# A hybrid decoder trunk on one core: GpSimd's 512-column subtractions in the gate/up units issued as two of 256

## What is computed

```
def swiglu(h, w_gu, w_down):
    gate, up = jnp.split(h @ w_gu, 2, axis=-1)
    return (jax.nn.silu(gate) * up) @ w_down

x = x + 0.5 * swiglu(rmsnorm(x, n1), ffn1_gu, ffn1_down)
... (mixer: gated linear attention and sliding-window attention)
x = x + 0.5 * swiglu(rmsnorm(x, n2), ffn2_gu, ffn2_down)
```

## Time and profile before

| | |
|---|---|
| time, median of 3 | 2162.82 us (2158.97 to 2165.57) |
| the profiled execution's own time | 2163.97 us |
| its span, first to last instruction | 2162.2 us |
| mean granted TensorE clock | 0.976 |
| PE, DVE, ACT, POOL busy | 95%, 66%, 39%, 45% of the span |
| POOL's 512-column subtractions (L535) | 360: 278.0 + 200.4 + 63.1 us busy |

### The profile page before, as it was taken

One profiled execution on the slowest core, in us unless ns is written; L12 is line 12 of the kernel. 1 busy time (PEld: TensorE's weight loads), 2 busy tenths in 40 slices (PEclk: granted clock), 3 DMA queues, 4 the chain that ended last, 5 costly groups with the idle time before them and its releaser, 6 DMA issues.

```text
span 2162.2 us, 41578 instructions
## 1 busy us (share of the span) xinstructions
PE 2044.2 (95%) x15854; PEld 1989.8 (92%) x15854; DVE 1425.0 (66%) x1853; ACT 846.8 (39%) x1469; POOL 980.0 (45%) x549
## 2 busy tenths in 40 slices
PE   6899999999999999999999999999999998999996
PEld 6899999998889999999998999999898998999996
DVE  8899932386348899952288997226754498999323
ACT  4455532235233445542235555222541334555321
POOL 3466654332203366664426666444321134666541
PEclk9999999999879999999999999999997999999998
DMA  3322242421212322242223222423220213222421
GB/s 121 124 93 92 82 153 94 133 79 50 81 52 71 114 88 92 92 143 98 97 74 125 92 88 99 143 95 127 69 91 30 68 63 134 88 92 78 159 98 61
DMA packets 86277, 206.74 MB, mean 96 GB/s; under 512 B 12240, under 2 KB 13936, under 8 KB 85616
## 3 DMA queue, kind: packets, MB, share of 16 engines
q1 hardware_dynamic: 78336, 192.06, 26.5%
q10 hardware_dynamic: 7824, 13.01, 1.8%
HBM read 191.20 MB, written 15.86 MB: 96 GB/s over the span
## 4 chain that ended last, share of the span: by engine, by line
issue 51%; PE 18%; POOL 16%; DVE 10%; DMA 2%; ACT 1%; DVEq 1%; POOLq 0%; SPq 0%; ACTq 0%
PE ps L565 13%; POOL w_lo L527 11%; POOL w_lo L535 6%; PE ps L591 5%; DVE ps L1356 3%; DMA w_raw<-stream 1%; DVE act L1391 1%; DVE b_tmp L1401 1%; DVE ssum L1447 1%; DVE s_tmp L1356 1%; DVE g_buf L1420 1%; DVE rs L1318 0%; DVE rhs L1413 0%; DVE b_tmp L1405 0%; DVE ssum L1458 0%
## 5 line engine op out<-in xcount | busy, mean ns | idle before, releaser
L591 PE MATMUL ps<-rhs,w_hi 128*128 128x272 f32 x4032 | 782.9, 291 | 54.3 <-DVE ssum L1447 46.8
L527 POOL TENSOR_TENSOR w_lo<-w_raw,w_hi 128x1024 fp32r<-128x1024 f32 x184 | 445.2, 2421 | 830.5 <-ACT w_hi L976 816.3
L591 PEld LDWEIGHTS ps<-rhs,w_hi 128*128 128x128 f32 x4032 | 640.5, 189 | 70.3 <-DVE ssum L1447 53.4
L591 PE MATMUL ps<-rhs,w_lo 128*128 128x272 f32 x2016 | 583.1, 289 | 0.0
L565 PE MATMUL ps<-act,w_hi 128*128 128x272 f32 x2816 | 467.2, 287 | 0.0
L535 POOL TENSOR_TENSOR w_lo<-w_raw,w_hi 128x512 fp32r<-128x512 f32 x180 | 278.0, 1552 | 306.2 <-ACT w_hi L1005 306.2
L976 ACT ACTIVATE w_hi<-w_raw 128x1024 fp32r<-128x1024 f32 x180 | 190.1, 1057 | 562.6 <-PE ps L565 503.6
L565 PEld LDWEIGHTS ps<-act,w_hi 128*128 128x128 f32 x2816 | 397.1, 188 | 0.0
L591 PEld LDWEIGHTS ps<-rhs,w_lo 128*128 128x128 f32 x2016 | 382.6, 190 | 0.0
L565 PE MATMUL ps<-h_mid,w_hi 128*128 128x272 f32 x1728 | 306.3, 296 | 4.4 <-DVE g_buf L1375 2.8
L565 PE MATMUL ps<-act,w_lo 128*128 128x272 f32 x1408 | 292.9, 289 | 0.0
(11 more groups left out here) (253 smaller groups left out, 2741.9 us busy)
## 6 DMA issues: line engine op xcount, KB each, us to landing
w_raw<-stream SPq DMA_DIRECT2D x184, 512.0 KB, 3.3
w_raw<-stream SPq DMA_DIRECT2D x252, 256.0 KB, 2.7
rs<-stream SPq DMA_DIRECT2D x36, 256.0 KB, 2.6
x_park<-x_end SPq DMA_DIRECT2D x16, 272.0 KB, 4.9
x_mid<-x_park SPq DMA_DIRECT2D x16, 272.0 KB, 4.9
x_park<-x_mid SPq DMA_DIRECT2D x16, 272.0 KB, 4.7
x_end<-x_park SPq DMA_DIRECT2D x16, 272.0 KB, 5.2
x_end<-xT ACTq DMA_DIRECT2D x8, 272.0 KB, 5.8
```

Of the source, the lines that this page charges most:

```text
L527: pool.tensor_tensor(w_lo[:, p % RING, :], w_raw[:, p % RAW, :], w_hi[:, p % RING, :].bitcast(F32), ALU.subtract).then_inc(lo_ready, 1)
L591: ins = pe.matmul(bank(v, at), w[:, k * P:(k + 1) * P], rhs[half][:, k, x, r, :], start=fresh and k == 0 and w is hi and x == 0, stop=k == ...
```

## The change

Each of POOL's subtractions in a unit is issued as two, columns 0 to 255 and 256 to 511. Only the first of a pair stands behind a wait, only the second raises the semaphore, so nobody sees the first half alone.

```diff
@@ unit_low, POOL's program
                 for op in POOL_LOW:
                     j = OPS.index(op)
                     pool.wait_ge(op_high, n * 7 + (j + 1))
-                    pool.tensor_tensor(operand(w_lo, j), source(op, v, half), operand(w_hi, j).bitcast(F32),
-                                       ALU.subtract).then_inc(pool_low, 1)
+                    for part in (slice(0, WB // 2), slice(WB // 2, WB)):
+                        ins = pool.tensor_tensor(operand(w_lo, j)[:, part], source(op, v, half)[:, part],
+                                                 operand(w_hi, j)[:, part].bitcast(F32), ALU.subtract)
+                    ins.then_inc(pool_low, 1)
```

## The result

| | before | after |
|---|---|---|
| time, median | 2162.75 us (2158.97 to 2165.57) | 2106.35 us (2104.57 to 2108.12) |
| profiled execution: time, span | 2163.97, 2162.2 us | 2108.12, 2106.3 us |

The ratio is 0.974, with a 95% interval of 0.9722 to 0.9759: 56 us faster. The forecast was 2101, range 2094 to 2142.

What follows compares the result with a forecast made beforehand. The bound was a loop of DVE's left_up to v_made, lengthened by turns with POOL, and PE's last two products. Windows gave -60.2 us and window 0 -2.7, total -62.9 from 2163.97; forecast 2101, range 2094 to 2142.

Steps and rivals of the forecast that it cites:

- The mechanism: In the units, DVE's two-SBUF-input operations wait for one POOL instruction, delaying v_made and PE; halves cut the hold to 0.54 us.
- 64 windows by 11.51 - 10.57: Main term: each of 64 windows, 16 a half, shortens by 0.94 us to PE's own 10.57, -60.2 us in all.
- Window 0's -2.7: First window of each half: L1391's wait for a POOL subtraction falls from 0.88 to 0.2 us, four times -0.68.
- the steady state: DVE's waits once shorter windows move POOL against DVE: first operation waits some 0.3 us, next three 0.54 each.
- Both values are below: 6.9 and 7.15 us from left_up to v_made were both below 7.30, so PE would no longer wait.
- The stretch: Time on DVE from the start of left_up to the end of v_made: 8.20 us before, forecast 6.9, or 7.15.
- The deadline: Latest end of v_made on DVE that spares PE a stall, put at 7.30 us after left_up.
- the thin margin: Room between the forecast end of v_made and PE's need: 0.15 to 0.4 us, a small miss costing little.
- 1 (no handing over between halves): DVE waits for both POOL halves at three operations a window: +0.57 us each window, 2200 us; chance 0.07.
- 2 (the fixed 0.18 us blocks as well): A POOL half holds DVE off 0.72 us; v_made comes after 7.6 to 7.9 us, 2129 to 2147; chance 0.14.
- 3 (POOL as the bound): POOL's loop passes 10.57 us if a half costs over 0.88 alone: 2105 to 2163 or slower; chance 0.04.
- 4 (another wait in its place, no change): In the units, another PE wait replaces the one for v_made, leaving 2163 us; chance 0.05.

Runs made afterwards that it cites:

- e1: The changed kernel with each POOL subtraction in the units cut into four of 128 columns instead of two: 2125.04 us, ratio 0.9831 to the kernel before.
- e3: The changed kernel with POOL's two pieces made 32 and 480 columns instead of equal halves: 2110.43 us, ratio 0.9759 to the kernel before.
- e7: The changed kernel with quarters of 128 columns and DVE's act_low moved ahead of the sum S3: 2105.16 us, ratio 0.9722 to the kernel before.
- e5: The changed kernel with DVE's act_low moved ahead of the sum S3: 2115.19 us, ratio 0.9778 to the kernel before.
- e9: The changed kernel with DVE's act_low moved behind v_made: 2095.43 us, ratio 0.9696 to the kernel before.

## Why the prediction was right, and where it was off

**The mechanism was right.** PE waited once a window for `v_made`, DVE was late because it and POOL take turns, one instruction each, and halves halved the turns. A contended DVE operation waits 0.52 to 0.55 us (1.21 to 1.25 less 0.69), forecast 0.54. A half costs 0.72 alone, forecast 0.72. L1393 rose from 0.71 to 1.25, as forecast. e1 and e3 confirm it at 128, 32 and 480 columns.

**The sum.** The forecast was -62.9 against the profiled execution; measured -55.9 (-56.4 by medians). The term that was mis-sized is "64 windows by 11.51 - 10.57", which measured 11.51 - 10.67 = 0.83 a window, 53.3 us instead of 60.2. Window 0's -2.7 stands beside some 2.4 us for the windows 0 and all that lies between the halves.

**The step that failed** is the steady state: 6.9 us to `v_made`, 7.15 at most, "Both values are below, so PE no longer waits". The stretch measured 7.26 to 7.32. I had let the sum S3 take its turn as soon as POOL's S3b was done. But it has a semaphore to wait for, since it overwrites POOL's source. In the kernel before POOL was done 2 us earlier and no wait showed. Now POOL is later by 0.19 us an operation and DVE is earlier. By the time DVE is told, POOL has begun A22a, and the sum waits 0.63 us for the semaphore and a whole turn after it. L1387 on the other hand waits hardly at all (0.02 to 0.06, forecast 0.3).

The deadline was off as well. It was put at 7.30 us; e7 with 7.01 us runs at PE's pace, the changed kernel with 7.26 to 7.32 loses 0.12. Where PE waits, the window was the stretch and 3.37 us (11.57 - 8.20 before, 10.64 - 7.26 after), so with PE's own pace of 10.55, not 10.57, the deadline is near 7.18. The stretch passed 6.9 us by 0.4 and the deadline by 0.1 only. That little was lost is the thin margin that the forecast named, and some luck: with quarters the same oversight cost 0.39 us a window.

The changed kernel's window also closes as a loop in which no step waits for PE. From the rows after: DVE's sum S4 ends at 182.52, POOL starts A12 at 184.04, ends S3 at 189.37, DVE's sum S3 starts at 189.44 and the next S4 ends at 193.16, 1.52 + 5.33 + 0.07 + 3.72 = 10.64 us. For quarters the same four give 10.94. Taking this loop away (e5) wasn't enough with halves, for a wait for ACT of the same size came in its place; taking `act_low` out of the stretch (e9) removed both.

**The rivals.** 1 (no handing over between halves): out, DVE gets in between. 2 (the fixed 0.18 us blocks as well): out, waits are 0.54 and not 0.72. 3 (POOL as the bound): POOL's working time isn't it (9.08 us busy in a window of 10.64), but the wait for its remainder of S3 was part of it, as said; with quarters that piece cost 0.39 us a window on PE's pace. 4 (another wait in its place, no change): out as stated, since PE waits for POOL's remainders in no steady window, and the wait that did appear cost 0.12 us a window and not 0.94.

## What to carry to other kernels

Where VectorE operations with two SBUF inputs stand on the critical path beside GpSimd work, cut the GpSimd instructions, not the GpSimd work: the wait is one instruction long. Before cutting finer, look for what waits for the end of the whole piece (here a sum that overwrites its source), since each cut makes that later. And an operation that nobody waits for belongs behind the signal that somebody waits for; here that alone gave 48 us, the cut alone 53 to 56, and both together 67.

## What the runs showed of the hardware

The time in which a GpSimd subtraction keeps a two-SBUF-input VectorE operation out is about 2.1 ns a column with no fixed part, at 32, 128, 256, 480, 512 and 1024 columns (about 0.06, 0.27, 0.54, 1.02, 1.08 and 2.2 us); the instruction's own 0.18 us (0.72 us alone less 0.54) pass beside VectorE's turn. A VectorE operation with one input in PSUM isn't kept out: 0.69 us beside GpSimd at work.

Executions of the same kernel differ by some us, and the difference goes with the mean granted clock of TensorE: over 30 executions of the kernel before, beside the experiments, from 0.973 (2167.98 us) to 0.979 (2158.50 us), each thousandth is worth some 1.4 us (a straight line through them). The clock is 1.00 in the windows of the units and lower in parts of the mixer: in the changed kernel's first profile 0.83 from 540 to 660 us and 0.85 from 1575 to 1680, with 0.53 from 620 to 630, near the lower level of 1.2 GHz. Its second profile has 0.82 and 0.80 there. The two have mean clocks of 0.977 and 0.972 and spans of 2106.3 and 2112.0 us, with the same windows of 10.67 us. A difference below some 5 us is better read from the length of a window than from the time.
